# One plain fp32 product in each gather, and a fifth weight unit loaded early, in a two-layer decoder kernel with a routed mixture of experts

## What is computed

```python
for layer in range(DEPTH):
    mix = conv_mla_mixer(x, ...) if layer % 2 == 0 else fox_mixer(x, ...)
    x = layer_norm(DN_ALPHA * x + mix, *ln1[layer])
    x = layer_norm(DN_ALPHA * x + moe(x, *moe_p[layer]), *ln2[layer])

def moe(x, router_w, ...):
    s = jax.nn.sigmoid(t @ router_w)            # t: 256 x 1024
    ...                                         # group-limited top 6, scaled gates
    def expert_step(acc, p):
        wg, wu, wd, g = p                       # 1024x256, 1024x256, 256x1024
        hid = jax.nn.silu(t @ wg) * (t @ wu)
        return acc + (hid @ wd) * g[:, None], None
    routed, _ = lax.scan(expert_step, ...)      # over 64 experts
    shared = (jax.nn.silu(t @ sh_w_gate) * (t @ sh_w_up)) @ sh_w_down
    return routed + shared
```

## Time and profile before

| | |
|---|---|
| median of 3 runs | 1226.66 us (1224.33 to 1228.28) |
| span of the profiled execution | 1227.7 us |
| TensorE busy | 1061.3 us (86%) |
| VectorE busy | 415.3 us (34%) |
| ScalarE busy | 233.2 us (19%) |
| DMA | 446.73 MB, 364 GB/s on average |

### The profile page before, as it was taken

The page is one execution under the profiler, slowest core; times in us unless marked ns, Lnnn a source line. Parts: engine busy times, 40 slices in busy tenths (PEclk is TensorE's granted clock), DMA queues, the critical chain, the costliest instruction groups (busy, mean ns, idle before and its releaser), DMA issues.

```text
span 1227.7 us, 19635 instructions
## 1 busy us (share of the span) xinstructions
PE 1061.3 (86%) x7794; PEld 624.9 (51%) x7794; DVE 415.3 (34%) x1023; ACT 233.2 (19%) x558; POOL 65.9 (5%) x100
## 2 busy tenths in 40 slices
PE   8999998889697997578899999988898879985775
PEld 5765664354444453344688747543444343543432
DVE  4855532223232232221345446232223232331213
ACT  2352321112121211011122224211121111110110
POOL 3141000000000000000132000000100000000000
PEclk9999999989898998789999999989899898998878
DMA  9258899999999999999991648999999999999995
GB/s 360 95 184 349 314 409 419 421 403 411 420 421 421 420 420 420 419 400 415 359 312 45 250 162 314 381 406 419 402 407 420 421 420 421 421 420 420 402 420 211
DMA packets 84829, 446.73 MB, mean 364 GB/s; under 512 B 8447, under 2 KB 26414, under 8 KB 37629
## 3 DMA queue, kind: packets, MB, share of 16 engines
q1 hardware_dynamic: 82214, 439.84, 88.7%
q0 software_dynamic: 2096, 5.47, 1.3%
q10 hardware_dynamic: 422, 0.08, 0.0%
HBM read 443.12 MB, written 1.05 MB: 362 GB/s over the span
## 4 chain that ended last, share of the span: by engine, by line
PE 60%; DMA 28%; SPq 4%; DVE 4%; issue 3%; ACT 1%; POOL 0%; DVEq 0%; ACTq 0%
DMA ring<-in_l_exp_w_down 15%; DMA ring<-in_l_exp_w_up 13%; PE bank L1252 12%; PE bank L1425 8%; PE bank L1463 5%; PE bank L1079 5%; PE bank L1001 4%; PE bank L1276 4%; PE bank L1288 3%; SPq L772 3%; PE bank L1082 2%; PE bank L1155 2%; PE bank L1396 2%; PE bank L1213 1%; PE bank L1381 1%
## 5 line engine op out<-in xcount | busy, mean ns | idle before, releaser
L1425 PE MATMUL bank<-ring,big 128*32 128x256 f32 x2816 | 181.2, 416 | 50.4 <-DMA ring<-in_l_exp_w_up 31.8
L1252 PE MATMUL bank<-ring,big 128*64 128x512 f32 x608 | 152.7, 635 | 43.3 <-DMA ring<-in_l_exp_w_up 43.3
L1425 PEld LDWEIGHTS bank<-ring,big 128*32 128x32 f32 x2816 | 99.6, 119 | 126.7 <-issue 64.3
L2331 DVE TENSOR_TENSOR mixT<-mixT,bank 128x512 f32<-128x512 f32 x120 | 78.5, 686 | 126.7 <-PE bank L1396 108.9
L1252 PEld LDWEIGHTS bank<-ring,big 128*64 128x64 f32 x608 | 48.4, 146 | 133.1 <-issue 132.4
L1463 PE MATMUL bank<-ring,big 128*32 128x512 f32 (+1 forms) x736 | 88.7, 623 | 20.4 <-DMA ring<-in_l_exp_w_down 17.0
L1288 PE MATMUL bank<-pick,xs_high 128*128 128x128 f32 x352 | 84.5, 282 | 0.0
L1288 PE MATMUL bank<-pick,xs_low 128*128 128x128 f32 x352 | 81.9, 275 | 0.0
L1288 PEld LDWEIGHTS bank<-pick,xs_high 128*128 128x128 f32 x352 | 67.6, 192 | 21.6 <-issue 21.6
L2301 DVE TENSOR_TENSOR big<-big,bank 128x256 f32<-128x256 f32 x22 | 9.3, 421 | 201.3 <-PE bank L1425 201.3
L1707 ACT ACTIVATE ys_high<-bank,gcol 128x512 fp32r<-128x512 f32 (+1 forms) x86 | 56.7, 677 | 95.6 <-PE bank L1276 50.9
(11 more groups left out here) (332 smaller groups left out, 1361.1 us busy)
## 6 DMA issues: line engine op xcount, KB each, us to landing
ring<-in_l_exp_w_gate SPq DMA_DIRECT2D x120, 1024.0 KB, 11.5
ring<-in_l_exp_w_up SPq DMA_DIRECT2D x120, 1024.0 KB, 16.2
ring<-in_l_exp_w_down SPq DMA_DIRECT2D x112, 1024.0 KB, 16.7
ring<-in_l_w_in SPq DMA_DIRECT2D x13, 1024.0 KB, 12.4
ring<-in_l_w_out SPq DMA_DIRECT2D x8, 1024.0 KB, 8.3
lead_par<-in_l_exp_w_down SPq DMA_DIRECT2D x6, 1024.0 KB, 12.1
ring<-in_l_exp_w_gate SPq DMA_DIRECT2D x12, 512.0 KB, 7.7
ring<-in_l_exp_w_up SPq DMA_DIRECT2D x12, 512.0 KB, 8.5
```

Of the source, the lines that this page charges most:

```text
L1252: ins = mm(ps[SLOTS * q:SLOTS * q + SLOTS, :], xg[:, c, SLOTS * j:SLOTS * j + SLOTS], both[:, c, 0:n:n - 1], start=(c == 0), stop=(c == C ...
L1425: ins = mm(ps[r, 0:HID], xn[:, c, r], loop_weights(L, j, w)[:, c, :], start=(c == 0), stop=(c == C - 1))
L2331: lp.done(v.tensor_tensor(part, part, ps[:], ALU.add), (of, n))
```

## The change

The rows are kept once, as plain fp32 (`xs`, in `side`), and each gather makes one plain product where two reduced ones were. The subtraction on VectorE is gone. ScalarE makes the second copy behind the router's sigmoid, not ahead of it. The place of `xs_low` in `V` takes a fifth lead unit, the gate unit of the fourth group's first expert. It is issued when attention and the convolution's layer norm have read `V` for the last time, ahead of the ninth early unit of the first group. As gate and up of that expert no longer lie side by side in the ring, its gate and up products of 512 columns become two of 256.

```diff
-LEAD = [(1, 2), (2, 2), (3, 2), (0, 2)]
+LEAD = [(1, 2), (2, 2), (3, 2), (0, 2), (0, 0)]
+LEAD_BEFORE = 8
...
+        lead_v = over("lead_v", "V", 0, [P, UNIT], F32)
-        xs = [over("xs_high", "side", 0, [P, TB, D], F32R), over("xs_low", "V", 0, [P, TB, D], F32R)]
+        xs = cut(side, 0, TB, D)
-        pick = over("pick", "side", 2048, [P, TB, GSLOT], F32R)
+        pick = cut(side, 2048, TB, GSLOT)
...
-                for j, w in (divmod(k, 3) for k in early):
+                for k in early:
+                    j, w = divmod(k, 3)
+                    if k == early[LEAD_BEFORE]:
+                        bank_read(sp, ("ot", L, 7 if L else 3))
+                        if L == 0:
+                            sp.wait_ge(S("u_normed"), TB)
+                        load_lead(*LEAD[4])
...
                     for tb in range(TB):
-                        for k in range(2):
-                            ins = mm(ps[:, 0:GSLOT], xs[k][:, tb, P * c:P * c + P], pick[:, tb, :],
-                                     start=(tb + k == 0), stop=(tb + k == 2))
+                        ins = mm(ps[:, 0:GSLOT], xs[:, tb, P * c:P * c + P], pick[:, tb, :], start=(tb == 0), stop=(tb == 1))
...
                             j = 2 * pr + q
+                            if in_lead(BEGIN[lp.kind] if lp.r is None else None, j, 0):
+                                for w in range(2):
+                                    ins = mm(ps[SLOTS * q:SLOTS * q + SLOTS, HID * w:HID * w + HID],
+                                             xg[:, c, SLOTS * j:SLOTS * j + SLOTS], loop_weights(L, j, w, LED)[:, c, :],
+                                             start=(c + w == 0), stop=(c + w == C))
+                                continue
...
-                for tb in range(TB):
+                def chunked(tb):
+
                     act.wait_ge(S("ln_done"), 4 * L + tb + 1)
-                    fn(by_piece(xs[0], tb), by_row(xrow, tb), ACT.Copy).then_inc(S("xs_high"), 1)
+                    fn(by_piece(xs, tb), by_row(xrow, tb), ACT.Copy).then_inc(S("xs"), 1)
+
+                chunked(0)
                 xt(1 + 2 * L, 2)
                 ps = bank_read(act, ("router", L))
                 bank_done(fn(sco, ps[:, 0:TB * NE].rearrange("p (a e) -> p a e", a=TB), ACT.Sigmoid), ("router", L))
+                chunked(1)
...
-                for tb in range(TB):
-                    if tb:
-                        xt(1 + 2 * L, (3,))
-                    dve.wait_ge(S("xs_high"), 2 * L + tb + 1)
-                    v.tensor_tensor(by_piece(xs[1], tb), by_row(xrow, tb), by_piece(xs[0], tb), ALU.subtract)\
-                     .then_inc(S("xs"), 1)
+                xt(1 + 2 * L, (3,))
```

More of the change, by code:

```diff
@@ L204, in plan_banks @@
         u.add(("pos", L), 0)
-        for c in range(C):
-            u.add(("gather", L, c), FIRST_GATHER[c])
+        for n in range(C):
+            u.add(("gather", L, n), FIRST_GATHER[n])
         wide = [("gT", 2)]
@@ L605, in loop_weights @@
                 n = LEAD.index((j, w))
-                a = lead_par[:, (n - 1) * UNIT:n * UNIT] if n else lead_rows
+                a = (lead_rows, *(lead_par[:, k * UNIT:k * UNIT + UNIT] for k in range(3)), lead_v)[n]
             return by_chunk(a) if w < 2 else by_pair(a)
@@ L1286, in pairs @@
                             for tb in range(TB):
-                                for k in range(2):
-                                    ins = mm(ps[:, n * s:n * s + n], xs[k][:, tb, P * (2 * c + s):P * (2 * c + s) + P],
-                                             pick[:, tb, 0:n], start=(tb + k == 0), stop=(tb + k == 2))
+                                ins = mm(ps[:, n * s:n * s + n], xs[:, tb, P * (2 * c + s):P * (2 * c + s) + P], pick[:, tb, 0:n],
+                                         start=(tb == 0), stop=(tb == 1))
                         lp.made(ins, ("pair", c))
```

## The result

| | median of the runs, us | lowest to highest, us | runs |
|---|---|---|---|
| before | 1226.67 | 1222.71 to 1231.91 | 22 |
| after | 1231.61 | 1226.28 to 1238.64 | 22 |

The ratio of after to before is 1.0039, with a 95% interval of 1.0026 to 1.0053. On 1226.7 us that is 4.8 us more (3.2 to 6.5).

What follows compares the result with a forecast made beforehand. The full stream of expert weights was taken as the bound, with its start, bytes and dry spells setting a layer's end. 2.8 - 2.5 + 0.6 + 0.9 + 0.2 = +2.0 us a layer, twice +4.0, gave 1230.7 us, range 1226 to 1237.

Steps and rivals of the forecast that it cites:

- The first gather: First group's gather on TensorE, ahead of gate and up: longer, starting the weight stream 2.8 us later in each layer.
- The pair gathers and the subtractions: Narrow groups' 128-column gathers and VectorE's removed subtractions before routing: 0 us more or less.
- The lead unit: Fifth unit loaded early into V: one unit less in the full stream, -2.5 us a layer, +0.6 of it lost.
- the short queue: Fourth group's loads, between down and up units: less cover without the gate unit, +0.6 us, bounds 0 and 1.1.
- The third group's wide gather: Ahead of the fourth group: grows by 2.0 to 2.4 us, hidden by TensorE's 3.49 us wait for weights.
- The split into two products: Fourth group's first expert, gate and up as two products of 256 columns: 0 us taken, up to 3.5 if not side by side.
- The later wide gathers: Fifth group's gather, partly on the path: +0.9 and +0.2 us a layer, bounds 0 and 2.6; later ones 0.
- near balance: Rival: the cheap ends hold, gain and loss of one size, +0.6 us a layer, 1228 us; chance 0.22.
- faster: Rival: plain product streams 256 columns as fast as the old pair, -5 us, 1221.7 us; chance 0.11.
- the later places bind fully: Rival: upper bounds hold, +4.4 us a layer, 1235.5 us; more than +8 us or a useless unit together had 0.12.
- the lead unit does nothing: Rival: its load is late or collides, +3.9 us a layer, 1234.5 us; with more than +8 us, chance 0.12.

Runs made afterwards that it cites:

- e11: Changed kernel with wide gathers as two reduced products of the high copy, pair gathers plain, lead unit kept: 1221.40 us, 0.9956 of before.
- e3: Changed kernel with all gathers as two reduced products of the high copy and no fifth lead unit: 1226.05 us, 0.9992 of before.
- e1: Changed kernel without the fifth lead unit, plain gathers kept: 1235.42 us, 1.0071 of before.
- e2: Changed kernel with every gather as two reduced products of the high copy, as long as the old pair, lead unit kept: 1223.02 us, 0.9968 of before.
- e7: Changed kernel with rows kept as two fp16 parts, two products a gather, and no fifth lead unit: 1224.17 us, 0.9983 of before.
- e4: Changed kernel with only the first group's gather as two reduced products, later gathers plain, lead unit kept: 1226.26 us, 0.9993 of before.
- e5: Changed kernel with the first gather plain, all later gathers as two reduced products, lead unit kept: 1228.62 us, 1.0016 of before.
- e8: Changed kernel with the gate unit of the fourth group's last expert as fifth lead instead of the first expert's: 1229.02 us, 1.0016 of before.
- e6: Changed kernel with rows kept as two fp16 parts, two products a gather, lead unit kept: 1221.37 us, 0.9947 of before.
- e10: Changed kernel with each gather as one reduced product of the high copy alone, lead unit kept: 1216.97 us, 0.9926 of before.

## Why the prediction was right

The forecast was 1230.7 us, slower, and 1231.61 was measured, the ratio giving +4.8 us where the sum was +4.0. Its steps, one by one:

- **The first gather, +2.8 us a layer.** Right, and a little small. The row is +3.1 (7.65 us, where I had said 7.4, against 4.56), near the upper bound of 3.16; the time gives 2.9. The chain has 4.56 + 2.79 = 7.35 us for products that take 6.91 by themselves, so of the 0.5 us of starts and bank waits, most of which I let shrink away, 0.44 are still there. (The old products start 0.12 us apart, not the 0.117 of my upper bound.)
- **The pair gathers and the subtractions, 0.** Right, by e11 and e3.
- **The lead unit, -2.5 + 0.6 = -1.9 us a layer.** Right as a sum, 1.9 in the mean of three pairs, but not shown as a mechanism. At 200 to 220 us layer 0 lost 1.3 us where I had 0.6 for the short queue (bound 1.1), but what of it the missing unit costs is not separated: over 180 to 220 us the changed kernel and e1, which has the unit in the queue, lose alike (1.5 and 1.6 us), while e2 loses 2.0 and e3 0.4. That the sum came out is luck: with the edit a stall at 510 to 560 us goes away, which I had not looked for. It costs 1.7 us a layer in the mean of e1, e3 and e7, and it follows a break in TensorE's work, not a lack of weights. Without that break in the kernel before, by the estimate above, the unit would have given far less than 1.9 us and the change would have cost more than +4.8. The unit landed at 114.9, not near 101: I had overlooked the units still on their way ahead of it; the DMA share is 1.01 from 95 to 110 us, before as well as after. It changed nothing, since the stream had room behind it (a DMA share of 0.72 over 120 to 140 us) and nobody reads the unit before 218.79.
- **The third group's wide gather, hidden.** Right. TensorE is last at the fourth group's start, and the products that took 8.70 us at a clock of 0.81 take 7.05 with the clock at 1.00. On the axis of before they start at 221.3 and end at 228.5, where I had 220.2 and 227.2, so 1.1 us of it is not hidden (227.35 before).
- **The split into two products, 0.** Right: 7.05 us.
- **The later wide gathers, +1.1 us a layer.** The term that is furthest off, with 1.5 by e4 and e5, though the spread of the times does not exclude 1.1. The mechanism held (the queue runs short behind the fifth group), but it was at 280 to 300 us that most was lost, 2.3 us in layer 0, later than the 265 to 285 that I wrote; 265 to 270 has its dip, 351 GB/s, in before already.

The direction is shown: the plain gathers cost 8.7 us with the lead unit there (e2). By the measured terms the layer is 2.9 - 1.9 + 1.5 = +2.5 us, twice +5.0, against +4.8 timed. Of the rivals, "near balance" and "faster" are outside the interval; "the later places bind fully" (+4.4 a layer) and "the lead unit does nothing" (+3.9 a layer) too; e1, without the unit, is at +8.7. But the last one is ruled out for the edit as a whole only: that the unit by itself does next to nothing, and the break is the gain, is not excluded.

What stays open: why TensorE's break, and with it the later stall, is gone in the kernels with the fifth lead unit, what the missing unit costs at 200 to 220 us, and what part of the 2.8 us between after and e8 is real.

## What to carry to other kernels

Before an edit's worth is put down to the idea behind it, look through the trace for breaks of the engines elsewhere that come or go with it: here one of 3.5 us, hundreds of microseconds behind the place of the edit.

Where a stream of weights is full, cost a change first by two things: when the stream starts to run full, and how many units it has to carry. Then look for the places where its queue is short: there the time of TensorE's releases counts, and with it the granted clock. Price a product from a row with the same type and the same width: one plain fp32 product took 1.8 times a reduced pair at 256 columns (0.432 against 0.24 us) and as long as the pair at 128 (0.226 against 0.24). If rows must be picked with more than one part's precision in the room of one fp32 copy, two fp16 parts and a one-hot matrix take less of TensorE's time than either kind here; how exact the picked rows are, no run here measures.

## What the runs showed of the hardware

- A plain fp32 product took 0.432 us at 256 columns and 0.226 at 128. Reduced ones start 0.12 us apart at both widths, fp16 ones 0.11 and 0.056 (in e6, twenty from 133.77 to 135.84 and sixteen from 191.54 to 192.39). For the reduced one 128 columns are no cheaper than 256.
- Plain fp32 products in the two halves of the array's columns run side by side even where one is 512 columns and the others are 256: 7.05 us for what takes 7.02 unsplit.
- The same sixteen records of the first projection took 5.8 us in eight of the thirteen profiles and 7.8 to 8.4 in five (before, e1, e6, e8, e11), with no change in the code. Windows of 2 us over this stretch have the granted clock at 1.00 before and after; the cause is open. A difference of 2.6 us between two single profiles can come from there; it is cut out by comparing from a later common point.
- TensorE stopped for 2.3 to 3.5 us once in each layer, in the middle of a run of products with no wait in the program between them, in all four kernels without the fifth lead unit (before, e1, e3, e7) and in none of the other nine, save 0.7 us in e10. In `prof`'s waits it stands as "issue". The cause is open.
